# Seven-product pairs of the down projection regrouped: runs of five, one inside a body, five and three, with GpSimd's products placed behind the third body

## The chip, the cores and the metric

One core of one Trainium2 chip. The metric is the device time of one execution in microseconds; the time of a kernel is the median of its runs.

## The reference, cut to what matters

The reference is one block of a hybrid encoder on 256 rows of 2048 columns in float32. The part that the change touches is its last stage, the down projection of the gated MLP with the residual and the final norm:

```
n2 = rmsnorm(x, norm_ffn_g)
gate, up = split(n2 @ w_up, 2)              # w_up: 2048 x 11264
gate = causal_dwconv(gate, ffn_conv_w, ffn_conv_b)
x = x + (silu(gate) * up) @ w_down          # w_down: 5632 x 2048
y = rmsnorm(x, norm_final_g)
```

## The kernel before, in words

**Tiles.** The down projection multiplies an activation of 44 tiles of 128 contraction rows (`act`, 256 columns of the sequence each) by `w_down` (44 tiles x 2048 columns). It goes over two halves of 1024 output columns. All products are made of a high and a low part: ScalarE rounds a tile to the high part, VectorE subtracts it from the source and gets the low part, and TensorE multiplies high by high, high by low and low by high.

**Bodies and pairs.** Of the 44 tiles, 16 go as four *bodies* of four *units*; a unit is one tile, a load of 512 KB (128 x 1024), one rounding of 128x1024 and one of 128x256 on ScalarE, one subtraction of each on VectorE, and 12 matmuls 512 columns wide. The other 28 tiles go as 14 *pairs* of two tiles each, done as a two-by-two block product with seven products in place of eight (`pair`, L1649), so 21 matmuls of 512 columns. A pair loads three plain weight blocks (256 and 512 KB, L428 and L429) and four weight sums that an earlier stage had stored in DRAM (`sums`, 1024 KB, L436). ScalarE rounds them in four pieces (`pair_hi`: plain blocks 128x1536, activations 128x896, two pieces of sums 128x1024 each, T1 and T2), and VectorE makes the four low parts in the same order (`pair_lo`, L1222), counting `s_lo_ready`. Call the pairs of one half q0 to q13.

**Places.** There are two sets of buffers. Place 0 is a pair's own: `s_raw` for loads, `s_w` for parts of weights, `s_act` for parts of activations. Place 1 is `raw`, `w` and `aT`, which the bodies use as a ring of four slots. Each buffer is single. The plain load of the next pair at a place waits until the first low part of the pair there before is made, the load of its sums waits for all four, and ScalarE's roundings wait for TensorE (`s_used`, which a pair counts after its third and its last product).

**Order.** Everything is in program order on each engine: SyncE issues the loads, ScalarE, VectorE and TensorE work in this order for each half: body 0, q0 to q6 at places 0, 1, 0, 1, 0, 1, 0, bodies 1 and 2, q7 to q13 at places 0, 1, 0, 1, 0, 1, 0, body 3. A wait of SyncE holds back the loads behind it. The transfers of one queue share 16 DMA engines.

**Work beside it.** In the second half ScalarE makes a Sqrt table load (`warm_sqrt`) and two squares of 128x1024 (`squares`, rows 0 and 1 of the first half's columns) between bodies 1 and 2. GpSimd waits for the last product of q6 in the second half, loads `gfin` (the gain of the final norm, spread to all partitions, 1024 KB in SBUF), and makes two products of 128x512 for each of two rows (`xg`, L1414). Those of row 0 wait for the third unit of body 1, those of row 1 for the third unit of body 2. Behind the last body come `pairs_out`, the residual, and the final norm's last scalings and stores.

Of the kernel before, what the change touches and what calls it, by code (L numbers as in the profile page):

```python
# [69 lines left out]
LAST_BODY = 0, 2  # L70
# [62 lines left out]
def hybrid_block(nc, x, w_in, w_out, w_up, w_down, wa, wx, gate_w, par_in, const_in, gfin_in, out):  # L133
    with ExitStack() as ctx:
# [152 lines left out]
        def at_start(run):  # L287

            return isinstance(run, int) and run == 0

        def place_of(i):

            return i % 2

        def nth_there(half, run, i):

            return (run + half * RUNS) * ((RUN_PAIRS + 1 - place_of(i)) // 2) + i // 2

        def nth_pair(half, run, i):

            return run * RUN_PAIRS + (half * PAIRS + i)
# [53 lines left out]
        def _(sp):  # L355
# [56 lines left out]
            def load_pair(half, run, i):  # L412

                place, p = place_of(i), nth_pair(half, run, i)
# [6 lines left out]
                if i == 1:  # L421
                    g = LAST_BODY[run] + (G_DOWN + half * DOWN_BODIES)
                    sp.wait_ge(lo_ready, g * RING + (RING + 2))
                elif i:
                    sp.wait_ge(s_lo_ready, p * S_PARTS + (1 - 2 * S_PARTS))
                elif half or not at_start(run):
                    sp.wait_ge(s_lo_ready, p * S_PARTS + (1 - S_PARTS))
                sp.dma_start(dst[:, 0:BANK], upper).then_inc(plain_landed[place], 16)  # L428
                sp.dma_start(dst[:, BANK:BANK + HALF], lower).then_inc(plain_landed[place], 16)  # L429
                if i == 1:  # L430
                    sp.wait_ge(lo_ready, g * RING + 2 * RING)
                elif i:
                    sp.wait_ge(s_lo_ready, p * S_PARTS - S_PARTS)
                elif half or not at_start(run):
                    sp.wait_ge(s_lo_ready, p * S_PARTS)
# [80 lines left out]
            def load_pairs(half, run):  # L516

                for i in range(RUN_PAIRS):
                    load_pair(half, run, i)
# [19 lines left out]
        def _(act_e):  # L539
# [205 lines left out]
            def prepare_body(src, group, first, pair_before=None):  # L745

                for s in range(RING):
# [7 lines left out]
            def pair_hi(half, run, i):  # L755

                place, p, nth = place_of(i), nth_pair(half, run, i), nth_there(half, run, i)
                g = LAST_BODY[run] + (G_DOWN + half * DOWN_BODIES)
                src, dst = pair_raw[place], pair_w[place]
                act_e.wait_ge(plain_landed[place], nth * S_LOADS + S_LOADS)  # L760
                if i == 1:
                    act_e.wait_ge(unit_used, g * RING + (RING + 2))
                elif i:
                    act_e.wait_ge(s_used, p * S_STEPS + (1 - 2 * S_STEPS))
                elif half or not at_start(run):
                    act_e.wait_ge(s_used, p * S_STEPS + (1 - S_STEPS))
# [3 lines left out]
                if i == 1:  # L770
                    act_e.wait_ge(unit_used, g * RING + 2 * RING)
                elif i:
                    act_e.wait_ge(s_used, p * S_STEPS - S_STEPS)
                elif half or not at_start(run):
                    act_e.wait_ge(s_used, p * S_STEPS)
# [10 lines left out]
            def down():  # L786

                for half in range(2):
                    g0 = G_DOWN + half * DOWN_BODIES

                    for i in range(RUN_PAIRS):
                        pair_hi(half, 0, i)
                    prepare_body(act, g0 + 1, RUN_SLOTS, nth_pair(half, 0, RUN_PAIRS - 2))
                    if half == 1:
                        warm_sqrt(A4)
                        for r in range(ROWS):
                            squares(A4, r, 0, V4)
                    prepare_body(act, g0 + 2, ACT_SLOTS - 2 * RING)
                    for i in range(RUN_PAIRS):
                        pair_hi(half, 1, i)  # L800
                    prepare_body(act, g0 + 3, ACT_SLOTS - RING, nth_pair(half, 1, RUN_PAIRS - 2))
# [60 lines left out]
        def _(dve):  # L862
# [345 lines left out]
            def split_body(src, group, first, count):  # L1208

                for s in range(RING):  # L1210
# [3 lines left out]
            def pair_lo(half, run, i):  # L1214

                place, p = place_of(i), nth_pair(half, run, i)
# [30 lines left out]
            def down():  # L1247

                for half in range(2):
# [5 lines left out]
                    for i in range(RUN_PAIRS):  # L1255
                        pair_lo(half, 0, i)
                    split_body(act, g0 + 1, RUN_SLOTS, tiles + RING)
                    split_body(act, g0 + 2, ACT_SLOTS - 2 * RING, tiles + 2 * RING)
                    for i in range(RUN_PAIRS):
                        pair_lo(half, 1, i)  # L1260
# [122 lines left out]
        def _(pool):  # L1383
# [35 lines left out]
        def _(pe):  # L1419
# [191 lines left out]
            def body(where, b, **ends):  # L1611
                for s in range(RING):
# [24 lines left out]
            def pair(half, run, i, opens=False, closes=False):  # L1637

                place, p = place_of(i), nth_pair(half, run, i)
# [15 lines left out]
            def down():  # L1655

                for half in range(2):
# [8 lines left out]
                    for i in range(RUN_PAIRS):  # L1666
                        pair(half, 0, i, opens=i == 0)
# [81 lines left out]
```

## Time and profile before

| what | value |
|---|---|
| median of 3 runs | 1121.95 us (1118.27 to 1122.04) |
| the profiled execution's own time | 1120.69 us |
| its span (first to last instruction) | 1118.9 us |
| TensorE busy in the span | 1102.7 us (99%) |
| VectorE, ScalarE, GpSimd busy | 875.7, 623.9, 50.9 us |
| down projection on TensorE | 882.63 to 1108.95 us of the span |
| mean DMA rate over the span | 263 GB/s |

Times inside the span are counted from its first instruction. The span is 1.8 us shorter than the execution's own time. A matmul's end in the trace is modelled, so one instruction's length overlaps the next one's; distances between starts are what counts.

### The profile page before, as it was taken

The numbers are of one execution on the slowest core, as the hardware profiler recorded it, in microseconds if no ns is written. First come the engines' busy times: TensorE is split into PE (matmuls) and PEld (weight loads), VectorE is DVE, ScalarE is ACT, GpSimd is POOL, SyncE is SP. The second block draws the span as 40 slices with busy tenths as digits, with TensorE's granted clock in tenths as the row PEclk, the third lists the DMA queues.
The fourth block names the chain that finished last, engine by engine and source line by source line (L and its number), as shares of the span: only waits on it lengthen the run. The fifth ranks groups of instructions, "written<-read, shape, count | busy, mean of one in ns | idle before, by whom it ended". The sixth has DMA issues, their size and how long they took to land.

```text
span 1118.9 us, 16379 instructions
## 1 busy us (share of the span) xinstructions
PE 1102.7 (99%) x5938; PEld 947.1 (85%) x5938; DVE 875.7 (78%) x1144; ACT 623.9 (56%) x794; POOL 50.9 (5%) x46
## 2 busy tenths in 40 slices
PE   8999999999999999999999999999999999999996
PEld 8888888888888888888888888888888877888875
DVE  6778587685875687788788778877876897999897
ACT  7656474564755664444444444444344676867774
POOL 0100000000000000000000000000000000000200
PEclk9999999999999999999999999999999999999998
DMA  8877878678566468889889888898898898879893
GB/s 257 250 217 249 244 223 255 203 237 260 173 224 206 154 221 269 262 286 296 288 272 288 294 277 268 289 291 281 272 299 292 284 330 300 323 276 326 315 317 140
DMA packets 186727, 293.94 MB, mean 263 GB/s; under 512 B 9228, under 2 KB 151824, under 8 KB 182976
## 3 DMA queue, kind: packets, MB, share of 16 engines
q1 hardware_dynamic: 185664, 291.15, 80.1%
q0 software_dynamic: 448, 1.78, 0.5%
q10 hardware_dynamic: 576, 0.53, 0.1%
q8 instruction: 20, 0.33, 0.1%
q14 instruction: 19, 0.16, 0.0%
HBM read 261.96 MB, written 31.46 MB: 262 GB/s over the span
## 4 chain that ended last, share of the span: by engine, by line
PE 77%; DVE 10%; DMA 8%; ACT 2%; issue 1%; SPq 0%; DVEq 0%; ACTq 0%
PE ps L1465 39%; PE ps L1467 20%; PE ps L1600 10%; PE ps L1649 3%; DVE s_w L1222 3%; DVE w L868 3%; DMA s_raw<-sums 3%; DMA s_raw<-w_down_dram 2%; PE ps L1462 2%; DMA raw<-w_up_dram 1%; PE ps L1463 1%; DVE w L1222 1%; ACT w L543 1%; ACT s_w L543 1%; DMA xres<-x_dram 1%
## 5 line engine op out<-in xcount | busy, mean ns | idle before, releaser
L1465 PE MATMUL ps<-xT,w 128*128 128x512 f32 x2048 | 716.6, 396 | 0.0
L1467 PE MATMUL ps<-xT,w 128*128 128x256 f32 x2048 | 569.4, 278 | 0.0
L543 ACT ACTIVATE w<-raw 128x1024 fp32r<-128x1024 f32 (+3 forms) x377 | 392.8, 1058 | 315.7 <-PE ps L1467 151.0
L868 DVE TENSOR_TENSOR w<-raw,w 128x1024 fp32r<-128x1024 f32 x332 | 405.1, 1239 | 181.2 <-ACT w L543 180.5
L1465 PEld LDWEIGHTS ps<-xT,w 128*128 128x128 f32 x2048 | 384.2, 188 | 90.5
L1467 PEld LDWEIGHTS ps<-xT,w 128*128 128x128 f32 x2048 | 384.8, 188 | 0.3
L1600 PE MATMUL ps<-w,aT 128*128 128x512 f32 x768 | 175.7, 389 | 0.0
L1600 PEld LDWEIGHTS ps<-w,aT 128*128 128x128 f32 x768 | 143.9, 188 | 29.9
L1649 PE MATMUL ps<-s_w,s_act 128*128 128x512 f32 x336 | 80.1, 393 | 3.0 <-DVE s_act L1222 3.0
L1649 PEld LDWEIGHTS ps<-s_w,s_act 128*128 128x128 f32 x336 | 62.7, 188 | 18.4 <-DVE s_act L1222 5.0
L543 ACT ACTIVATE fs<-fc 128x512 f32<-128x512 f32 x22 | 13.9, 633 | 105.9 <-DVE fc L1307 105.9
L1222 DVE TENSOR_TENSOR s_w<-s_raw,s_w 128x1024 fp32r<-128x1024 f32 (+1 forms) x48 | 66.9, 1420 | 7.7 <-ACT s_w L543 7.6
L543 ACT ACTIVATE s_w<-s_raw 128x1024 fp32r<-128x1024 f32 (+1 forms) x48 | 55.8, 1194 | 17.1 <-DMA s_raw<-sums 8.9
L1649 PE MATMUL ps<-w,aT 128*128 128x512 f32 x252 | 59.5, 391 | 0.1
L1649 PEld LDWEIGHTS ps<-w,aT 128*128 128x128 f32 x252 | 47.0, 188 | 10.9 <-DVE aT L1222 1.1
L1405 POOL TENSOR_TENSOR fs<-fs,rB 128x512 f32<-128x512 f32 x22 | 29.3, 1331 | 568.3 <-ACT fs L543 568.3
L1222 DVE TENSOR_TENSOR w<-raw,w 128x1024 fp32r<-128x1024 f32 (+1 forms) x36 | 50.4, 1427 | 1.3 <-ACT w L543 1.1
L1052 DVE TENSOR_TENSOR s_raw<-s_raw 128x512 f32<-128x512 f32 x56 | 38.4, 687 | 0.7
L1307 DVE SCALAR_TENSOR_TENSOR fc<-fg,par,fc 128x256 f32<-128x256 f32 x88 | 36.7, 479 | 0.0
L1049 DVE TENSOR_TENSOR s_raw<-s_raw 128x1024 f32<-128x1024 f32 x28 | 34.1, 1218 | 0.0
L1462 PE MATMUL ps<-w,xT 128*128 128x512 f32 x96 | 34.1, 399 | 0.0
L543 ACT ACT_TABLE_LOAD x23 | 29.5, 1283 | 2.7 <-issue 2.3
(177 smaller groups left out, 629.1 us busy)
## 6 DMA issues: line engine op xcount, KB each, us to landing
raw<-w_up_dram SPq DMA_DIRECT2D x176, 512.0 KB, 5.9
raw<-w_in_dram SPq DMA_DIRECT2D x92, 512.0 KB, 4.3
s_raw<-w_down_dram SPq DMA_DIRECT2D x72, 512.0 KB, 7.8
sums<-s_raw SPq DMA_DIRECT2D x56, 512.0 KB, 6.5
raw<-w_down_dram SPq DMA_DIRECT2D x44, 512.0 KB, 6.7
raw<-w_out_dram SPq DMA_DIRECT2D x32, 512.0 KB, 4.6
s_raw<-sums SPq DMA_DIRECT2D x16, 1024.0 KB, 7.2
raw<-sums SPq DMA_DIRECT2D x12, 1024.0 KB, 7.3
```

The lines of the kernel that those rows point to most:

```text
L543: return sc.activation(out_, in_, fn, **kw)
L868: v.tensor_tensor(w[:, s, :, 1, :], raw[:, s, :].rearrange("p (c n) -> p c n", c=CH), w[:, s, :, 0, :], ALU.subtract).then_inc(lo_ready, 1)
L1049: v.tensor_tensor(t_out[:, 0:2, :], t_raw[:, 0:1, :].to_broadcast([P, 2, BANK]), t_raw[:, 1:3, :], ALU.subtract).then_inc(t_summed, 1)
L1052: v.tensor_tensor(t_out[:, n + 1, :], t_raw[:, n + 1, :], t_out[:, 2 * n - 2, :], ALU.subtract).then_inc(t_summed, 1)
L1222: v.tensor_tensor(out_, in_, hi, ALU.subtract).then_inc(s_lo_ready, 1)
L1307: did(v.scalar_tensor_tensor(out=fc[:, b, :], in0=tap, scalar=fpar(b, k), in1=fc[:, b, :], op0=ALU.mult, op1=ALU.add), V3, f"c{b}_{k}")
L1405: did(nc.gpsimd.tensor_tensor(fs[:], fs[:], rB[:].to_broadcast([P, 2, S]), ALU.mult), L3, "fs_r")
L1462: mm(full, xT[:, kt, 0, cut], w[:, s, c, :, :].rearrange("p a n -> p (a n)"), start=kt == 0, stop=False)
L1465: mm(full, w[:, s, c, 0, cut], xT[:, kt, :, :].rearrange("p a n -> p (a n)"), start=kt == 0, stop=False)
L1467: ins = mm(rest, w[:, s, c, 1, cut], xT[:, kt, 0, :], start=False, stop=kt == KT - 1)
L1600: ins = mm(ps[:, bank0 + 2 * r + n, :], aT[:, s, a_part, cut], w[:, s, 2 * n:2 * n + 2, w_part, :], start=opens and s == 0 and a_part == 0 ...
L1649: ins = mm(ps[:, bank, :], pair_act[place][:, a_part, cut], pair_w[place][:, m, w_part, :], start=opens and not plain and a_part == 0 and ...
```

## The change

The 14 pairs of a half are no longer two runs of seven. The order becomes: body 0, q0 to q4, units 0 and 1 of body 1, q5, units 2 and 3 of body 1, q6 to q10, body 2, q11 to q13, body 3. The places become 0, 1, 0, 1, 0, 0, 0, 1, 0, 1, 0, 0, 1, 0, so that q5 follows q4 at place 0, q6 follows q5 there, and q11 follows q10 there. SyncE issues the loads of all four units of body 1 ahead of those of q5 to q10. The number of pairs, units, loads and matmuls stays. In the second half the Sqrt table load and the square of row 0 now stand between the roundings of q5 and those of units 2 and 3; the square of row 1 stands behind these, ahead of q6. GpSimd's wait for the load of `gfin` keeps its count (the last product of q6), which now comes later in the half; its products of row 0 wait for unit 0 of body 2 and those of row 1 for unit 2 of body 2.

```diff
+HALF_PLACES = 0, 1, 0, 1, 0, 0, 0, 1, 0, 1, 0, 0, 1, 0
+FIRST_IN_RING = {1: 0, 7: 1, 12: 2}
+LAST_IN_RING = {1: 3, 2: 9, 3: 12}
...
+        def pair_there_before(half, q):
+            same = [n for n in range(2 * PAIRS) if n < nth_pair(half, q) and place_of(n % PAIRS) == place_of(q)]
+            return same[-1]
...                                                     (SyncE)
-                load_pairs(half, 0)
-                load_body(g0 + 1, w_down, RUN_TILES, half, nth_pair(half, 0, RUN_PAIRS - 2))
-                load_body(g0 + 2, w_down, FT - 2 * RING, half)
-                load_pairs(half, 1)
-                load_body(g0 + 3, w_down, FT - RING, half, nth_pair(half, 1, RUN_PAIRS - 2))
+                load_pairs(half, 0, 4)
+                load_body(g0 + 1, w_down, RUN_TILES, half, nth_pair(half, LAST_IN_RING[1]))
+                load_pairs(half, 5, 10)
+                load_body(g0 + 2, w_down, FT - 2 * RING, half, nth_pair(half, LAST_IN_RING[2]))
+                load_pairs(half, 11, 13)
+                load_body(g0 + 3, w_down, FT - RING, half, nth_pair(half, LAST_IN_RING[3]))
...                                                     (ScalarE; VectorE and TensorE likewise)
-                    for i in range(RUN_PAIRS):
-                        pair_hi(half, 0, i)
-                    prepare_body(act, g0 + 1, RUN_SLOTS, nth_pair(half, 0, RUN_PAIRS - 2))
+                    for q in range(0, 5):
+                        pair_hi(half, q)
+                    prepare_body(act, g0 + 1, RUN_SLOTS, nth_pair(half, LAST_IN_RING[1]), (0, 1))
+                    pair_hi(half, 5)
                     if half == 1:
                         warm_sqrt(A4)
-                        for r in range(ROWS):
-                            squares(A4, r, 0, V4)
-                    prepare_body(act, g0 + 2, ACT_SLOTS - 2 * RING)
-                    for i in range(RUN_PAIRS):
-                        pair_hi(half, 1, i)
+                        squares(A4, 0, 0, V4)
+                    prepare_body(act, g0 + 1, RUN_SLOTS, nth_pair(half, LAST_IN_RING[1]), (2, 3))
+                    if half == 1:
+                        squares(A4, 1, 0, V4)
+                    for q in range(6, 11):
+                        pair_hi(half, q)
+                    prepare_body(act, g0 + 2, ACT_SLOTS - 2 * RING, nth_pair(half, LAST_IN_RING[2]))
+                    for q in range(11, 14):
+                        pair_hi(half, q)
...                                                     (GpSimd)
-                pool.wait_ge(unit_used, (G_DOWN + DOWN_BODIES + r + 1) * RING + (RING + 3))
+                pool.wait_ge(unit_used, (G_DOWN + DOWN_BODIES + 2) * RING + (RING + 1 + 2 * r))
```

## Rows read from the trace of the kernel before

**Rows 1.** The page, busy time of each engine over the span.
```profile
PE 1102.7 (99%) x5938; PEld 947.1 (85%) x5938; DVE 875.7 (78%) x1144; ACT 623.9 (56%) x794; POOL 50.9 (5%) x46
```

**Rows 2.** Windows: stretch and its length, busy time by engine, clock, DMA share, GB/s.
```profile
893.53:929.32 35.79, 34.22 (x148) 27.36 (x147) 33.97 (x30) 28.89 (x31) 0.00 (x0) 1.00 0.90 314
929.32:951.08 21.76, 21.76 (x97) 18.02 (x96) 16.11 (x18) 11.89 (x15) 0.00 (x0) 1.00 0.92 312
951.08:984.59 33.51, 33.51 (x149) 27.60 (x147) 31.07 (x27) 27.92 (x29) 0.00 (x0) 1.00 0.86 310
1006.35:1040.69 34.34, 34.12 (x148) 27.44 (x147) 32.00 (x27) 27.75 (x29) 0.00 (x0) 1.00 0.90 312
1062.47:1097.91 35.44, 34.16 (x148) 27.35 (x147) 33.74 (x28) 28.03 (x30) 1.66 (x1) 1.00 0.89 308
```

**Rows 3.** Timeline of TensorE, pairs that it waited for: start, length, and the wait.
```profile
913.59 5.09 PE L1649 MATMUL ps<-s_w,s_act 128*128 128x512 f32 x21 [0.76 <-DVE s_act L1222]
...
924.39 5.09 PE L1649 MATMUL ps<-s_w,s_act 128*128 128x512 f32 x21 [0.81 <-DVE s_act L1222]
...
1083.05 5.08 PE L1649 MATMUL ps<-s_w,s_act 128*128 128x512 f32 x21 [1.28 <-DVE s_act L1222]
```

**Rows 4.** The chain of waits in the second half's first run: start, length.
```profile
1017.17 7.06 DMA s_raw<-sums
...
1027.74 7.36 DMA s_raw<-sums
```

**Rows 5.** DMA issues from 880 us on: count, KB each, median us to landing.
```profile
s_raw<-sums SPq DMA_DIRECT2D x15, 1024.0 KB, 7.1
...
s_raw<-w_down_dram SPq DMA_DIRECT2D x15, 512.0 KB, 7.1
s_raw<-w_down_dram SPq DMA_DIRECT2D x15, 256.0 KB, 5.3
...
act<-gfin_dram POOLq DMA_DIRECT2D x1, 1024.0 KB, 8.7
```

**Rows 6.** Line L436, loads of sums between 900 and 1050 us.
```profile
DMA to landing us min/median/max: 4.8/7.3/12.1
```

**Rows 7.** Timeline of VectorE, second half: start, length.
```profile
1032.96 1.76 DVE L1222 TENSOR_TENSOR s_w<-s_raw,s_w 128x1536 fp32r<-128x1536 f32 x1
1034.63 1.08 DVE L1222 TENSOR_TENSOR s_act<-act,s_act 128x896 fp32r<-128x896 f32 x1
1036.21 2.36 DVE L1222 TENSOR_TENSOR s_w<-s_raw,s_w 128x1024 fp32r<-128x1024 f32 x2 [0.49 <-ACT s_w L543]
1038.49 1.22 DVE L868 TENSOR_TENSOR w<-raw,w 128x1024 fp32r<-128x1024 f32 x1
1039.62 0.42 DVE L874 TENSOR_TENSOR aT<-act,aT 128x256 fp32r<-128x256 f32 x1
...
1059.50 3.46 DVE L1222 TENSOR_TENSOR s_w<-s_raw,s_w 128x1024 fp32r<-128x1024 f32 x2
1062.88 2.86 DVE L1222 TENSOR_TENSOR w<-raw,w 128x1536 fp32r<-128x1536 f32 x1
```

**Rows 8.** Timeline of ScalarE, both halves: start, length.
```profile
942.05 1.49 ACT L543 ACTIVATE s_w<-s_raw 128x1536 fp32r<-128x1536 f32 x1 [0.23 <-DMA s_raw<-w_down_dram]
...
1035.12 2.01 ACT L543 ACTIVATE s_w<-s_raw 128x1024 fp32r<-128x1024 f32 x2 [1.35 <-DMA s_raw<-sums]
1037.03 1.04 ACT L543 ACTIVATE w<-raw 128x1024 fp32r<-128x1024 f32 x1
...
1042.16 1.28 ACT L543 ACT_TABLE_LOAD   x1
...
1044.79 1.06 ACT L543 ACTIVATE act<-xres 128x1024 f32<-128x1024 f32 x1
...
1055.30 1.49 ACT L543 ACTIVATE s_w<-s_raw 128x1536 fp32r<-128x1536 f32 x1 [1.71 <-DMA s_raw<-w_down_dram]
```

**Rows 9.** Timeline of GpSimd, the second pair of products.
```profile
1060.07 4.06 POOL L1414 TENSOR_TENSOR act<-xres,act 128x512 f32<-128x512 f32 x2 [6.58 <-PE ps L1600]
```

More of the change, by code:

```diff
@@ L410, in store_sums, with load_pair @@
                     sp.dma_start(dst[part], s_raw[:, (2 + part) * HALF:(3 + part) * HALF]).then_inc(t_stored, 16)
-            def load_pair(half, run, i):
-                place, p = place_of(i), nth_pair(half, run, i)
+            def load_pair(half, q):
+                run, i = divmod(q, RUN_PAIRS)
+                place = place_of(q)
                 cols = half * HALF
@@ L514, in _, with load_pairs @@
             sp.wait_ge(t_stored, 32 * 2 * PAIRS)
-            def load_pairs(half, run):
-                for i in range(RUN_PAIRS):
-                    load_pair(half, run, i)
+            def load_pairs(half, first, last):
+                for q in range(first, last + 1):
+                    load_pair(half, q)
             for half in range(2):
                 g0 = G_DOWN + half * DOWN_BODIES
-                load_pairs(half, 0)
-                load_body(g0 + 1, w_down, RUN_TILES, half, nth_pair(half, 0, RUN_PAIRS - 2))
-                load_body(g0 + 2, w_down, FT - 2 * RING, half)
-                load_pairs(half, 1)
-                load_body(g0 + 3, w_down, FT - RING, half, nth_pair(half, 1, RUN_PAIRS - 2))
+                load_pairs(half, 0, 4)
[4 more added lines that the diff above has]
+                load_body(g0 + 3, w_down, FT - RING, half, nth_pair(half, LAST_IN_RING[3]))
                 if half == 0:
@@ L743, in _, with prepare_body @@
             head(H - 1, True)
-            def prepare_body(src, group, first, pair_before=None):
-                for s in range(RING):
+            def prepare_body(src, group, first, pair_before=None, units=range(RING)):
+                for s in units:
                     if pair_before is not None:
@@ L1206, in add_residual, with split_body, pair_lo @@
                                     xres[:, r, lo:hi], ALU.add), V, f"out{r}_{n}")
-            def split_body(src, group, first, count):
-                for s in range(RING):
+            def split_body(src, group, first, count, units=range(RING)):
+                for s in units:
                     split_units(group, [s])
                     split_tiles(src, first, count, [s])
-            def pair_lo(half, run, i):
-                place, p = place_of(i), nth_pair(half, run, i)
+            def pair_lo(half, q):
+                run, i = divmod(q, RUN_PAIRS)
+                place, p = place_of(q), nth_pair(half, q)
                 src, dst = pair_raw[place], pair_w[place]
@@ L1609, in half_unit, with body @@
                     ins.then_inc(unit_used, 1)
-            def body(where, b, **ends):
-                for s in range(RING):
+            def body(where, b, units=range(RING), **ends):
+                for s in units:
                     for r in range(ROWS):
@@ L1635, in out_products, with pair @@
                     last_body(where, OUT_BODIES - 1, late if half == 1 else None)
-            def pair(half, run, i, opens=False, closes=False):
-                place, p = place_of(i), nth_pair(half, run, i)
+            def pair(half, q, opens=False, closes=False):
+                place, p = place_of(q), nth_pair(half, q)
                 bank0 = 4 * (1 - half)
@@ L1665, in down @@
                         after(pe, V4, "out1_0")
-                    for i in range(RUN_PAIRS):
-                        pair(half, 0, i, opens=i == 0)
-                    body(where, 1)
+                    for q in range(0, 5):
+                        pair(half, q, opens=q == 0)
+                    body(where, 1, (0, 1))
+                    pair(half, 5)
+                    body(where, 1, (2, 3))
+                    for q in range(6, 11):
+                        pair(half, q)
                     body(where, 2)
-                    for i in range(RUN_PAIRS):
-                        pair(half, 1, i, closes=i == RUN_PAIRS - 1)
+                    for q in range(11, 14):
+                        pair(half, q, closes=q == PAIRS - 1)
                     if half == 0:
```

73 lines of the change are left out of this document (33 added, 40 removed).

## The prediction

> **What bounds the kernel now.** The page comes first, for the engine that fills the span: TensorE is busy 99% of it [rows 1], so a new order of the same matmuls can only win back time in which TensorE waits. The windows then say how much that is in the down projection. A run of seven pairs without any wait takes 33.51 us, 4.79 us for a pair; two bodies take 21.76 us, 2.72 us for a unit. The other three runs of seven take 35.79, 34.34 and 35.44 us [rows 2]: 2.28, 0.83 and 1.93 us too long, together 5.04 us. The change cannot win more there, and 5.04 us is 0.45% of 1121.95 us. About 0.5% is what a measurement of this kernel can tell from no change, so a gain that can be measured is nearly shut out before any step is costed.
>
> The timeline of TensorE says where the 5.04 us sit: ahead of the fifth and the seventh pair of a run, both at place 0, and the low parts of the activations come last [rows 3]. The chain of waits says why. At place 0 the loads of sums follow each other from 1017.17 to 1027.74 [rows 4]: one round of load, rounding and subtraction takes 10.57 us, while TensorE needs 9.57 us for two pairs. The load itself is 7.06 to 7.36 us of that [rows 4], against 4.8 us at the fastest [rows 6], so it queues. Two pairs load 2 x 1792 KB, 3.67 MB, which in 9.57 us is 383 GB/s; the runs of pairs get 308 to 314 GB/s at a DMA share near 0.9 [rows 2, 5]. A run of pairs therefore lives on a lead that it eats at some 1.1 us per two pairs, and a body (2 MiB in 10.88 us, 193 GB/s) gives it back.
>
> I measure this by lateness: when a pair's last low part is made, counted from the pair's start on TensorE. The next pair needs 1.67 + 1.00 us of VectorE (the distances between starts and the end of its first two low parts [rows 7]) within 4.79 us, so waits begin at a lateness of about 2.1 us. In the second half's first run it is 1.25 us at q2 (1017.17 against 1006.35 + 9.57), 2.24 at q4 and 3.5 at q6 (1038.57 against 1035.07) [rows 2, 4, 7], and the waits start behind q4.
>
> **Up to q5.** Nothing changes before q4's start except that the ring's loads beside q4 and q5 are 1024 KB ahead of the second megabyte where a pair's plain loads were 768 KB. In the first half q4 still starts at 913.59, 0.91 us later than 893.53 + 4 x 4.79 [rows 2, 3]. That wait stays. Then units 0 and 1 (5.44 us) stand where a pair (4.79 us) stood, and q5 follows at place 0 just as the seventh pair did, so the old seventh pair's dates serve for q5. First half: due at 913.59 + 4.79 + 5.44 = 923.82, old start 924.39 [rows 3], a wait of 0.57 us. Second half: due at 1006.35 + 5 x 4.79 + 5.44 = 1035.73, low part ready at 1034.63 + 1.08 = 1035.71 [rows 7], no wait. The 256 KB more cost 0 (nothing queued) to 0.8 us (0.26 MB at 312 GB/s) in each half; I take 0.2, near zero, because the extra load is queued eight microseconds ahead of q5's sums.
>
> **The table load and the square inside body 1.** In the second half they now stand between q5's last rounding and unit 2's. Before, they stood behind a body that was already prepared, and 10 us of matmuls hid them. Now ScalarE ends q5's sums at 1035.12 + 2.01 = 1037.13, the table load and the square take 2.63 us (1042.16 to the second square at 1044.79), unit 2's rounding 1.04, VectorE's two low parts 1.55 (1038.49 to 1040.04) [rows 7, 8]: unit 2 is ready at 1042.4, with the 0.2 of above at 1042.6. TensorE ends q5 at 1035.73 + 0.2 + 4.79 = 1040.7. That is a new wait of 1.9 us. It is 0 if q5's sums land after 4.8 us instead of 7.36 [rows 4, 6], and with a full 0.8 us of queueing it is still 1.9, since both sides move. I take 1.9, because q5's sums are queued behind the same loads as the seventh pair's were.
>
> The trace shows the table load as 1.28 us, with the next activation at its end [rows 8]. The Trainium skill (ScalarE: Activation LUTs, "What ACT_TABLE_LOAD costs") adds a drain of about 1.38 us to every switch; by it the new wait would be 3.3 us and the sum 1.4 us higher. The row has no such gap, and the row is used.
>
> **q6 to q10.** Place 0 has now no long pause from q0 to q10. Behind q5 the queue is short, which helps: q5's four low parts are made at 1038.57, q6's sums land between 1043.4 (4.8 us) and 1045.9 (7.36 us), and one rounding and two subtractions later (some 3.4 us) its low parts are complete between 1046.8 and 1049.3. q6 is due at 1035.73 + 4.79 + 5.44 = 1045.96, so its lateness is 0.9 to 3.4 us. Two rounds at 1.1 us each follow (q8, q10), and all above 2.1 us becomes wait: 1.0 us at the fast end, 2.3 us when the lateness starts at the threshold, which it can't pass without having waited already. I take 1.0 us in each half, since the queue has just run empty (in the second half the wait at unit 2 gives the loads more time, and the second square of 1.06 us [rows 8] takes some of it back).
>
> **The load of gfin.** It is issued when q6 has ended. Before, two bodies began there, and place 0 was merely late: its plain blocks were rounded 14.61 us after the bodies' start (1055.30 against 1040.69, which is 1006.35 + 34.34), 12.73 us in the first half without this load (942.05 against 929.32) [rows 2, 8]. Nobody on TensorE waited. Now it lands in q7 to q10, where the queue decides. It costs nothing if the lateness were below 2.1 us minus its delay, 3.3 us if its 1024 KB simply take their time at 312 GB/s [rows 2, 5]. I take the 1.9 us by which it delayed place 0.
>
> **GpSimd's products.** In the old order the second two (4.06 us) [rows 9] ran beside the low parts of the run's first two pairs: two subtractions of VectorE took 3.46 and 2.86 us where 2.36 and 1.76 are usual [rows 7], 1.1 us more each. The fifth pair of that run then came 1.28 us late [rows 3], and the run lost 1.93 us; the same run in the first half lost none [rows 2]. In the new order three pairs follow, then a body. VectorE has to make units 0 to 3 (4 x 1.48), q11 (5.0) and absorb some 3.6 us of contention in body 2's 10.88 us, coming from a lateness near 3: q11 ends up with a lateness of some 2.4, 0.3 us over the threshold. I take 0.3, with 0 and the old 1.93 as bounds. The Trainium skill (SBUF — State Buffer, "Who interferes with whom") says that a VectorE operation with two SBUF inputs and a GpSimd one that reads SBUF exclude each other for a whole instruction; the trace agrees, as 1.1 us steps rather than a general slowing show. The first half's last three pairs: no wait.
>
> **The sum.** First half: 0.91 + 0.57 + 0.2 + 1.0 = 2.7 us (now 2.28). Second half: 0.2 + 1.9 + 1.0 + 1.9 + 0.3 = 5.3 us (now 2.76). Together 8.0 against 5.04: 3.0 us more. The tail keeps its length, as GpSimd's products end more than a body ahead of their use. The profiled execution's own 1120.69 would become 1123.7; the median of the runs, 1.26 us above it, becomes 1124.9.
>
> The Trainium skill (DMA: Bandwidth & Descriptors, "Specifications") gives some 358 GB/s as one core's limit from HBM. By it a round of two pairs would be 10.25 us, the loss 0.7 in place of 1.1 us, and the sum an estimated 1.5 us lower. The windows show at most 314 GB/s in pairs.
>
> **Rivals.** (A) The forecast: new waits in the second half (square, gfin) outweigh the shorter runs; 1124.9. Chance 0.48.
> (B) The shorter runs win: sums land in 4.8 us behind each body, so unit 2 and q6 to q10 don't wait, and gfin is covered. Left are 0.91 + 0.57 and half a microsecond or so in each half, 2.5 us: 1119.4. For it: the run of seven that follows two bodies loses nothing [rows 2]. Against it: only 2.72 x 2 us of body now stand between q4, q5 and q6. Chance 0.30.
> (C) All waits go, even q4's: 1121.95 - 5.0 = 1116.9. Nothing before q4 changes, which speaks against it. Chance 0.07.
> (D) Slower by more than 0.5%: gfin's megabyte meets a queue with no slack, every later load of q7 to q10 is 3.3 us late and both rounds fall to 2.3 us of wait, and the lateness carries into q11, which then loses the 1.9 us again. 1.7 + 2.3 in the first half, 0.2 + 1.9 + 2.3 + 3.3 + 1.9 in the second: 13.6 us, 8.6 more, 1130.5. It decides once q10's sums land more than some 2.6 us later than in A. Chance 0.15.
>
> So the range is 1118.0 to 1129.0. Faster by over 0.5% (below 1116.3) needs C and luck: 0.04. Slower by over 0.5% (above 1127.6) is most of D: 0.14. Within 0.5%: 0.82.
>
> **What would show it.** In the profile after: q4 of the first half waiting as before; TensorE idle ahead of unit 2 of body 1 in the second half, released by a low part that waited for ScalarE; waits in q8 to q10 larger in the second half than in the first, with a load of sums of over 8 us beside gfin; no wait ahead of q13 in the second half. The prediction is wrong if the second half's q5 to q10 pass without waits, or if place 0, which now carries q4, q5 and q6 in a row, waits for its own roundings where I found them covered.

## Result: 0.3% slower, and the profile after

| | runs | median us | range us |
|---|---|---|---|
| kernel before | 12 | 1119.64 | 1116.62 to 1122.04 |
| changed kernel | 12 | 1121.69 | 1120.22 to 1126.30 |

The ratio is 1.0031, 95% interval [1.0017, 1.0045], so 3.5 us more; the two medians themselves are 2.1 us apart. A second set of runs of the same kernel gave 1.0042 [1.0025, 1.0058]. That is clear of noise and within half a per cent. The profiled execution took 1120.22 us with a span of 1118.4 us, a little less than before's. The page's span doesn't show the loss: in this execution the down projection took 1.8 us longer, but the stages ahead happened to end 1.8 us sooner, and what follows body 3's start took 20.4 us in place of 21.0.

The page of the changed kernel, the engines' busy time, answers to [rows 1]:
```profile
PE 1100.9 (98%) x5938; PEld 946.9 (85%) x5938; DVE 875.8 (78%) x1144; ACT 623.8 (56%) x794; POOL 51.5 (5%) x46
```
The same instructions, the same busy time. Only windows over the down projection show a difference. The columns are those of [rows 2]; the stretches are q0 to q4, body 1 with q5 in it, and q6 to q10 of the first half; body 1 with q5, q6 to q10, and q11 to q13 of the second:
```profile
891.77:915.71 23.94, 23.94 (x106) 19.72 (x105) 22.84 (x20) 18.28 (x19) 0.00 (x0) 1.00 0.94 333
915.71:932.22 16.51, 15.98 (x71) 12.87 (x69) 12.78 (x12) 11.39 (x13) 0.00 (x0) 1.00 0.71 249
932.22:957.07 24.85, 24.22 (x106) 19.64 (x105) 22.55 (x20) 20.74 (x22) 0.00 (x0) 1.00 1.00 368
...
1028.04:1044.53 16.49, 15.97 (x71) 12.82 (x70) 11.34 (x11) 15.11 (x19) 0.00 (x0) 1.00 0.75 262
1044.53:1072.70 28.17, 24.70 (x107) 19.44 (x105) 24.41 (x22) 20.94 (x23) 0.58 (x1) 1.00 0.95 340
...
1083.58:1097.97 14.39, 14.39 (x64) 11.83 (x63) 14.39 (x13) 12.33 (x15) 1.77 (x1) 1.00 0.65 221
```
Five pairs without a wait take 23.94 us, a pair with four units 15.67 us. The second and third stretch of each half carry it: 0.84 and 0.91 us lost in the first half, 0.82 and 4.23 us in the second. Read the DMA columns with them. Around q5 the DMA engines are 0.71 busy and move 249 GB/s, where two whole bodies had 0.92 and 312 GB/s [rows 2]; in the five pairs behind, they are 1.00 busy and move 368 GB/s. So the pause inside body 1 is used only in part for loading, and the run behind it starts a queue that is full at once. The queue of SyncE shows why. Between the load of q5's sums and the first load of q6 it issues nothing for 8.2 us, because q6 needs q5's buffer and q5's first low part is ready only at 920.79:
```profile
912.63 0.33 SPq L436 DMA_DIRECT2D s_raw<-sums  x1
920.82 0.33 SPq L430 DMA_DIRECT2D s_raw<-w_down_dram  x1
```

The timeline of TensorE, start, length and wait:
```profile
921.85 5.09 PE L1657 MATMUL ps<-s_w,s_act 128*128 128x512 f32 x21 [0.53 <-DVE s_act L1226]
...
952.14 5.09 PE L1657 MATMUL ps<-s_w,s_act 128*128 128x512 f32 x21 [0.63 <-DVE s_act L1226]
...
1038.98 5.71 PE L1608 MATMUL ps<-w,aT 128*128 128x512 f32 x24 [0.52 <-DVE aT L877]
...
1062.83 5.04 PE L1657 MATMUL ps<-w,aT 128*128 128x512 f32 x21 [3.29 <-DVE aT L1226]
```
These are q5 and q10 of the first half, unit 2 of body 1 and q9 of the second half. The waits of [rows 3] at the seventh and the fifth pair are gone; these stand in their place. The timeline of ScalarE has the causes of the last two:
```profile
1033.75 1.28 ACT L544 ACT_TABLE_LOAD   x1
...
1035.16 1.04 ACT L544 ACTIVATE act<-xres 128x1024 f32<-128x1024 f32 x1
...
1036.20 1.04 ACT L544 ACTIVATE w<-raw 128x1024 fp32r<-128x1024 f32 x1
...
1038.71 1.04 ACT L544 ACTIVATE act<-xres 128x1024 f32<-128x1024 f32 x1
...
1058.49 1.49 ACT L544 ACTIVATE w<-raw 128x1536 fp32r<-128x1536 f32 x1 [2.36 <-DMA raw<-w_down_dram]
```
Unit 2 is rounded only at 1036.20, behind table load and square. q9's plain blocks are rounded only at 1058.49: their load is the late one. That load, 512 KB issued at 1048.35, took 10.1 us to land. DMA issues between 1049 and 1060 us, columns as in [rows 5]:
```profile
act<-gfin_dram POOLq DMA_DIRECT2D x1, 1024.0 KB, 10.1
raw<-sums SPq DMA_DIRECT2D x1, 1024.0 KB, 9.7
```
q9's sums took 9.7 us beside `gfin`, against the usual 7.1 to 7.3 [rows 5, 6]. (L1226 is the low parts of pairs, [rows 7]'s L1222; L1657 and L1608 are the matmuls of pairs and units.)

**How the loss is counted below.** From q0's start to body 3's start on TensorE, less the same work without waits, 88.78 us (14 x 4.787 + 8 x 2.72). All executions, by the starts in their timelines:

| execution | order of the half | first half lost | second half lost |
|---|---|---|---|
| before, shown above | old, old | 2.28 | 2.78 |
| before_again | old, old | 0.93 | 1.55 |
| before_products_early | old, old | 0.83 | 2.74 |
| before_gfin_at_q2 | old, old | 2.23 | 3.89 |
| changed | new, new | 1.79 | 5.09 |
| after_again | new, new | 1.72 | 5.34 |
| gfin_small | new, new | 2.73 | 3.38 |
| gfin_at_q4 | new, new | 2.97 | 3.17 |
| squares_late | new, new | 2.60 | 3.06 |
| both_moved | new, new | 2.79 | 3.14 |
| first_half_only | new, old | 3.28 | 2.56 |
| second_half_only | old, new | 0.99 | 5.45 |
| runs_5333 | own, own | 1.21 | 6.72 |
| sums_halved | new, new | 0.04 | 1.02 |

An execution's first half doesn't depend on what is changed in the second, so the first column holds five samples of the old order (mean 1.45, 0.83 to 2.28) and seven of the new one (mean 2.55, 1.72 to 3.28; sums_halved, which loads less, is not among them). The means differ by 1.1 us, with a standard error of some 0.4 us. One trace is one sample of a quantity that scatters by over 1 us, and most of the readings below rest on one trace of their kernel.

### The profile page after: what moved, and what is told of

The parts are those of the page before. It is cut to its first block, busy times and chain, and to the rows that moved or that the text cites. A ratio compares the mean times of both kernels' runs of the same rounds, so it can differ in the third digit from the quotient of the medians.

```text
span 1118.4 us, 16379 instructions
## 1 busy us (share of the span) xinstructions
PE 1100.9 (98%) x5938; PEld 946.9 (85%) x5938; DVE 875.8 (78%) x1144; ACT 623.8 (56%) x794; POOL 51.5 (5%) x46
## 4 chain that ended last, share of the span: by engine, by line
PE 80%; DVE 9%; DMA 7%; ACT 2%; SPq 1%; issue 0%; DVEq 0%; ACTq 0%
PE ps L1473 42%; PE ps L1475 21%; PE ps L1608 11%; DVE s_w L1226 3%; DVE w L1226 2%; DMA s_raw<-w_down_dram 2%; PE ps L1470 2%; PE ps L1657 2%; DMA raw<-w_down_dram 2%; DMA raw<-sums 1%; PE ps L1471 1%; DVE w L871 1%; ACT s_w L544 1%; DMA xres<-x_dram 1%; ACT w L544 1%; DVE s_act L1226 1%
## 5 line engine op out<-in xcount | busy, mean ns | idle before, releaser
L544 ACT ACTIVATE w<-raw 128x1024 fp32r<-128x1024 f32 (+3 forms) x371 | 385.8, 1056 | 309.5 <-PE ps L1475 166.3
L1608 PE MATMUL ps<-w,aT 128*128 128x512 f32 x768 | 176.4, 389 | 0.5 <-DVE aT L877 0.5
L1608 PEld LDWEIGHTS ps<-w,aT 128*128 128x128 f32 x768 | 143.8, 188 | 30.7 <-DVE w L871 0.9
L1657 PE MATMUL ps<-s_w,s_act 128*128 128x512 f32 x378 | 90.1, 393 | 1.3 <-DVE s_act L1226 1.2
L1657 PEld LDWEIGHTS ps<-s_w,s_act 128*128 128x128 f32 x378 | 70.6, 188 | 18.3 <-DVE s_act L1226 2.3
L1226 DVE TENSOR_TENSOR s_w<-s_raw,s_w 128x1024 fp32r<-128x1024 f32 (+1 forms) x54 | 75.5, 1425 | 12.3 <-ACT s_w L544 12.2
L544 ACT ACTIVATE s_w<-s_raw 128x1024 fp32r<-128x1024 f32 (+1 forms) x54 | 62.8, 1194 | 22.4 <-DMA s_raw<-w_down_dram 11.9
L1657 PE MATMUL ps<-w,aT 128*128 128x512 f32 x210 | 49.3, 390 | 3.3 <-DVE aT L1226 3.3
L1657 PEld LDWEIGHTS ps<-w,aT 128*128 128x128 f32 x210 | 39.3, 188 | 11.9 <-DVE aT L1226 3.7
L1226 DVE TENSOR_TENSOR w<-raw,w 128x1024 fp32r<-128x1024 f32 (+1 forms) x30 | 42.2, 1432 | 5.7 <-ACT w L544 5.7
```

The source lines that it names most:

```text
L544: return sc.activation(out_, in_, fn, **kw)
L1226: v.tensor_tensor(out_, in_, hi, ALU.subtract).then_inc(s_lo_ready, 1)
L1608: ins = mm(ps[:, bank0 + 2 * r + n, :], aT[:, s, a_part, cut], w[:, s, 2 * n:2 * n + 2, w_part, :], start=opens and s == 0 and a_part == 0 ...
L1657: ins = mm(ps[:, bank, :], pair_act[place][:, a_part, cut], pair_w[place][:, m, w_part, :], start=opens and not plain and a_part == 0 and ...
```

## Experiments

Each was timed in five rounds beside the kernel before, and profiled once. Sections of two kernels show the edit of each against its base, the changed kernel unless the name says before.

**after_again, before_again.** Both kernels once more.

> The changed kernel once more, for a second trace and for the scatter. Loss means the time from q0's start to body 3's start on TensorE, less 88.78 us (14 x 4.787 + 8 x 2.72). In the first trace it is 1.79 us in the first half and 5.09 us in the second, of which 3.3 us is one wait ahead of q9. Theory (the load of gfin in the middle of q7 to q10 costs what its megabyte takes): the second half again loses 4.5 to 5.5 us with one wait of about 3 us ahead of q9. Rival (that wait was a chance of one execution, as the first half's wait at q4 was): the second half loses 2 to 4 us and no wait is over 1.5 us. Time: 1 to 5 us over the kernel before.

Measured: 1.72 and 5.34 us lost, a wait of 2.48 us ahead of q9 in the second half. A further 1.7 us are lost inside q9, whose matmuls take 6.49 us from start to start (1062.71 to 1069.20) because its sums landed only after 9.5 us. From q8's start to q10's this trace lost 4.4 us, the first one 4.1. The theory holds, the wait belongs to the kernel.

> The kernel before once more, for a second trace and the scatter of this chip. In its first trace the loss from q0's start to body 3's start is 2.28 us in the first half and 2.78 us in the second. Theory (the waits belong to the order): the same waits at the seventh pair of the first runs and at the fifth pair of the second half's second run, 1.5 to 3 us in each half. Rival (scatter of the DMA queue): one half loses less than 0.8 or more than 4 us.

Measured: ratio 1.0002 [0.9992, 1.0012]; 0.93 and 1.55 us lost. There are two waits of half a microsecond, ahead of the seventh pair of the first half's first run, as in the first trace, and ahead of the seventh pair of the second half's second run, where the first trace had its wait at the fifth:
```profile
1090.05 5.09 PE L1649 MATMUL ps<-s_w,s_act 128*128 128x512 f32 x21 [0.51 <-DVE s_act L1222]
```
One half lies inside the theory's range and the other, at 0.93, below it but above the rival's 0.8; the order has its waits, but this execution lost 2.48 us in all where the first had lost 5.06. The trace that the prediction rests on was at the upper end.

**gfin_small, gfin_at_q4: the load of gfin.**
```diff
-            pool.dma_start(gfin, gfin_in.to_broadcast([P, D])).then_inc(gfin_landed, 16)
+            pool.dma_start(gfin[:, 0:64], gfin_in[:, 0:64].to_broadcast([P, 64])).then_inc(gfin_landed, 16)
```


> The changed kernel, but the load of gfin brings 64 of 2048 columns at the same place (32 KB in SBUF in place of 1024 KB), so the final gain is wrong in the rest of the columns; all else is the same. Theory (queue): the wait ahead of q9 goes, the second half loses 5.1 - 3.3 = 1.8 us, the time is that of the kernel before or up to 1.5 us less. Rival (lateness: place 0 has too little pause, and gfin only moved the wait to q9): the second half still loses 3.5 us or more, spread over q8 to q10, and the time falls by less than 1 us against the changed kernel.

Measured: ratio 1.0026 [1.0013, 1.0038], the second half lost 3.38 us. Its timeline still has q9:
```profile
1062.42 5.05 PE L1657 MATMUL ps<-w,aT 128*128 128x512 f32 x21 [1.94 <-DVE aT L1226]
```
The megabyte is 1.9 us of the 5.3 us lost (mean of the three executions with it, 5.09, 5.34 and 5.45), not 3.3. The theory fails by its number (1.8 us forecast for the second half) and the rival is nearer: a wait at q9 is there without the megabyte. In time the effect is 0.05 to 0.16%, inside the intervals.

```diff
-            pool.wait_ge(s_used, S_STEPS * (PAIRS + RUN_PAIRS))
+            pool.wait_ge(s_used, S_STEPS * (PAIRS + 5))
```


> The changed kernel with the full load of gfin issued after q4's last product in place of q6's, so that it lands beside units 0 and 1 of body 1 and q5, where the queue had run nearly empty. Theory (queue slack decides): it costs q6 0 to 1 us, the 3.3 us at q9 go, the second half loses 2 to 3 us. Rival (a megabyte costs its 3.3 us wherever place 0 is near its limit, and q5 and q6 have only 5.44 us of body between them): the wait moves to q5 or q6 and the second half loses 4.5 us or more.

Measured: ratio 1.0030 [1.0015, 1.0045], 3.17 us lost in the second half, no wait at q5 or unit 2; waits of 0.43 and 0.58 us ahead of q7 and q10 instead of the long one at q9, and one of 0.60 ahead of q13. A little above the forecast of 2 to 3 us; in this trace the load costs no more around q5 than a load that is hardly there. In time it can't be told from the changed kernel.

**squares_late, both_moved: ScalarE's table load and squares.**
```diff
-                    if half == 1:
-                        warm_sqrt(A4)
-                        squares(A4, 0, 0, V4)
                     prepare_body(act, g0 + 1, RUN_SLOTS, nth_pair(half, LAST_IN_RING[1]), (2, 3))
-                    if half == 1:
-                        squares(A4, 1, 0, V4)
                     for q in range(6, 11):
                         pair_hi(half, q)
                     prepare_body(act, g0 + 2, ACT_SLOTS - 2 * RING, nth_pair(half, LAST_IN_RING[2]))
+                    if half == 1:
+                        warm_sqrt(A4)
+                        for r in range(ROWS):
+                            squares(A4, r, 0, V4)
```


> The changed kernel with the Sqrt table load and both squares behind the roundings of body 2 (10.9 us of matmuls ahead of them), none in body 1. Theory (ScalarE's order): the 0.8 us around unit 2 of body 1 go; q6's low parts come some 1 us earlier; the load of gfin still costs its wait, so the second half loses about 4.3 us and the time is 1 us less than the changed kernel. Rival (the wait at unit 2 only delayed what waits later anyway): the 0.8 us turn up at q9 and the second half loses 5.0 us as before.

Measured: ratio 1.0018 [1.0006, 1.0030], the second half lost 3.06 us, 2.2 us less than the 5.3 us with them in body 1. There is no wait at unit 2, and q6's last low part is made 0.23 us ahead of its start, where it is 1.75 us behind it in the changed kernel. So the table load and the squares cost 2.0 us of lead besides the 0.8 us wait that they show: the lead decides how long the queue's shortage can be covered. With it, q9 passes although the whole gfin is loaded, and in q6 to q10 one wait is left, ahead of q10:
```profile
1066.00 5.10 PE L1656 MATMUL ps<-s_w,s_act 128*128 128x512 f32 x21 [1.85 <-DVE s_act L1225]
```
The theory's 4.3 us and the rival's 5.0 us were both above the 3.06 us measured. The net figure also hides a part of the price. Up to body 2 the second half lost 2.2 us here against 5.3, so 3.1 us were won; the last three pairs then lost 0.9 us (15.24 us in place of 14.36), which the changed kernel doesn't lose. The squares now stand ahead of q11's roundings, and two of its low parts run beside GpSimd's products:
```profile
1079.88 4.59 DVE L1225 TENSOR_TENSOR s_w<-s_raw,s_w 128x1024 fp32r<-128x1024 f32 x2
```
That is 2.2 us more than the usual 2.36, and q12 waits.

> The changed kernel with the load of gfin after q4 and the table load and the squares behind body 2's roundings. Theory (these two are the whole loss of the change): the second half loses 1.5 to 2 us, as the first does, and the time is 1 to 2 us under the kernel before. Rival (the regrouping itself costs in the second half): it still loses 3.5 us or more.

Measured: ratio 1.0015 [0.9999, 1.0031], 2.79 and 3.14 us lost, nearer to the rival than to the theory, and the time is 1.7 us over the kernel before where the theory had it 1 to 2 us under. By one trace each (3.17, 3.06 and 3.14 us), the two moves together win no more than either one alone: with gfin's load at q4, q6's lateness is back at 1.81 us, and the lead that the squares had given is gone. The ratios (1.0030, 1.0018, 1.0015) can't tell the three apart. What is left in the second half, 3.1 us, lies near the new order's first half (2.55), where neither gfin nor squares are.

**before_gfin_at_q2, before_products_early: the old order.**
```diff
-            pool.wait_ge(s_used, S_STEPS * (PAIRS + RUN_PAIRS))
+            pool.wait_ge(s_used, S_STEPS * (PAIRS + 3))
```


> The kernel before, with the load of gfin issued after q2's last product in the second half, inside the run of seven, in place of after q6 at the start of two bodies. Theory (the megabyte costs 2 to 3.3 us wherever it is put into a run of pairs, and nothing in front of bodies): the second half's first run loses 0.83 + 2 to 3.3 us, the time is 2 to 3 us over the kernel before. Rival (the 3.3 us in the changed kernel came from q4, q5 and q6 following each other at place 0): the run loses less than 1.8 us.

Measured: ratio 1.0016 [1.0004, 1.0027]. The second half's first run takes 37.13 us (1003.93 to 1041.06) in place of 34.34 [rows 2], a loss of 3.62 us, with waits inside q5 and ahead of q6:
```profile
1032.28 3.04 PE L1649 MATMUL ps<-w,aT 128*128 128x512 f32 x12 [1.62 <-DVE w L1222]
1036.14 5.08 PE L1649 MATMUL ps<-s_w,s_act 128*128 128x512 f32 x21 [0.82 <-DVE s_act L1222]
```
In the four executions with gfin's load behind q6, this run lost 0.83, 0.20, 1.73 and 0.09 us, 0.7 on average, so the megabyte costs some 2.9 us in a run of pairs of the old order too: the theory holds for the run, while the time is 1.8 us over the kernel before (0.4 to 3.0), just under the 2 to 3 us forecast. The second run, however, then loses only 0.25 us (1062.84 to 1096.60), although GpSimd's products still run beside its first pairs:
```profile
1060.43 4.03 POOL L1414 TENSOR_TENSOR act<-xres,act 128x512 f32<-128x512 f32 x2 [7.29 <-PE ps L1600]
```

```diff
-                pool.wait_ge(unit_used, (G_DOWN + DOWN_BODIES + r + 1) * RING + (RING + 3))
+                pool.wait_ge(unit_used, (G_DOWN + DOWN_BODIES + 1) * RING + (RING + 3 + r))
```


> The kernel before, with GpSimd's products of row 1 behind the last unit of body 1 in place of the third unit of body 2, so that they run right after those of row 0, beside the preparation of body 2 and not beside q7 and q8. Theory (contention of GpSimd's products with VectorE cost the second half's second run 1.93 us): this run loses 0 to 0.6 us and the time is 1.5 to 2 us under the kernel before. Rival (the run was late because its first loads had been behind gfin's): the run still loses 1.5 us or more although its subtractions have their usual length.

Measured: ratio 0.9997 [0.9985, 1.0009], no gain where 1.5 to 2 us were forecast. The second run still loses 1.0 us (1061.11 to 1095.62), between theory and rival, with all four products done 5 us before it begins:
```profile
1090.69 5.08 PE L1649 MATMUL ps<-s_w,s_act 128*128 128x512 f32 x21 [0.54 <-DVE s_act L1222]
```
With both the load of gfin ahead and the products beside it, this second run lost 1.93, 1.33 and 2.45 us (the kernel before twice, and first_half_only). With the products and without the load ahead it lost 0.25 us, with the load and without the products 1.0 us. Each of the last two is one trace, against a scatter of 1 us; but that the products alone cost the run its 1.93 us is not borne out. The traces put some half of it on them and more on the load, so that the megabyte is not free in front of bodies either. (Moving the load also put 3 us of waits into the run ahead; what these gave the second run in lead is not separated.)

**first_half_only, second_half_only: the new order in one half.** The orders, places and waits come from a list for each half (S0 and S1 are the squares, the table load goes with S0). The lists of first_half_only:
```diff
+ORDERS = ("p0 p1 p2 p3 p4 u4 u5 p5 u6 u7 p6 p7 p8 p9 p10 u8 u9 u10 u11 p11 p12 p13 u12 u13 u14 u15",
+          "p0 p1 p2 p3 p4 p5 p6 u4 u5 u6 u7 S0 S1 u8 u9 u10 u11 p7 p8 p9 p10 p11 p12 p13 u12 u13 u14 u15")
+PLACES = (0, 1, 0, 1, 0, 0, 0, 1, 0, 1, 0, 0, 1, 0), (0, 1, 0, 1, 0, 1, 0, 0, 1, 0, 1, 0, 1, 0)
```


> The new order in the first half alone; the second half, its squares and GpSimd's load and products as in the kernel before. Over the executions so far the first half lost 2.28, 0.93, 0.83 and 2.23 us in the old order (mean 1.6) and 1.79, 1.72, 2.73, 2.97, 2.60 and 2.79 us in the new one (mean 2.4). Theory (place 0 has no long pause from q0 to q10, so the wait only moves from the seventh pair to q10): the first half loses 2 to 3 us with a wait ahead of q10, the time is 0.5 to 1.5 us over the kernel before. Rival (the regrouping costs nothing; all the loss is gfin and the squares, in the second half): no more than 1.6 us lost there, time as before.

Measured: ratio 1.0002 [0.9987, 1.0016], 3.28 us lost in the first half, waits at q5, q7 and q9:
```profile
937.35 5.10 PE L1692 MATMUL ps<-w,aT 128*128 128x512 f32 x21 [0.90 <-DVE aT L1266]
...
948.15 5.09 PE L1692 MATMUL ps<-w,aT 128*128 128x512 f32 x21 [0.77 <-DVE aT L1266]
```
The trace says what the theory says, and a little more than its 3 us, though at q7 and q9 and not at q10; the time says the rival's. The interval reaches to 1.8 us, so the 1.1 us between the means of the table is not excluded, nor shown by the times.

> The old order in the first half, the new one with its squares and GpSimd's work in the second. Theory: the second half loses 5 us as in the two traces of the changed kernel (5.09 and 5.34), the first 0.8 to 2.3 us; the time is 2 to 3 us over the kernel before, most of the change's 3.5 to 4.5 us. Rival (half of the change's cost is the first half's): 1 to 1.5 us over.

Measured: ratio 1.0039 [1.0020, 1.0059], 0.99 and 5.45 us lost. By the times the slowdown is the second half's: 4.4 us, above the 2 to 3 us that the theory gave it, with an interval from 2.2 to 6.6.

**runs_5333: another grouping.** The edit against second_half_only, whose second half has the new order; the first half's list gets the same order.
```diff
-ORDERS = (... "p0 p1 p2 p3 p4 u4 u5 p5 S0 u6 u7 S1 p6 p7 p8 p9 p10 u8 u9 u10 u11 p11 p12 p13 ..."
+ORDERS = (... "p0 p1 p2 p3 p4 u4 u5 u6 p5 p6 p7 u7 u8 u9 S0 S1 p8 p9 p10 u10 u11 p11 p12 p13 ..."
-            pool.wait_ge(s_used, S_STEPS * (PAIRS + 7))
+            pool.wait_ge(s_used, S_STEPS * (PAIRS + 8))
-                pool.wait_ge(unit_used, unit_count(1, (8, 10)[r]))
+                pool.wait_ge(unit_used, unit_count(1, (10, 11)[r]))
```


> Both halves regrouped to body 0, q0 to q4, three units, q5 to q7, three units, q8 to q10, two units, q11 to q13, body 3, with the places 0 1 0, 0 1 0, 0 1 0 in the later runs; the squares and the load of gfin in the second gap of three units. Lateness theory (a round of 10.6 us at place 0 against 9.57 us between its pairs, 12.95 us across three units, 10.2 across two): lateness grows by at most some 2.1 us before a gap takes it back, against 3.1 in the old order and 4.8 in the changed one, so the first half loses 0 to 0.8 us and the time is 0 to 2 us under the kernel before. Rival (DMA supply of the whole stretch decides, not where the pauses stand): both halves lose as in the old order or more, the time is that of the kernel before or over it.

Measured: ratio 1.0048 [1.0032, 1.0064], so 5.4 us over the kernel before where the theory allowed 2: the rival has the time right. The first half lost 1.21 us, as little as the old order's mean and above the forecast; the second lost 6.72 us. The chain of waits there begins with the table load (1048.90) and the squares ahead of q8 and runs through q8, q10 and q11 of place 0:
```profile
1056.25 7.91 DMA s_raw<-w_down_dram
...
1067.86 7.56 DMA s_raw<-w_down_dram
...
1076.97 2.48 DVE s_w L1266
1079.46 2.10 DVE s_act L1266
1081.55 4.48 DVE s_w L1266 x2
```
Here GpSimd's products do cost time: q11's first two low parts take 4.6 us where 2.67 are usual, and TensorE waits for them. In this trace the contention is paid where the lead is gone.

**sums_halved: less to load.**
```diff
-                sp.dma_start(dst[:, 2 * HALF:4 * HALF], sums).then_inc(sums_landed[place], 16)
+                sp.dma_start(dst[:, 2 * HALF:3 * HALF], sums[:, 0:HALF]).then_inc(sums_landed[place], 16)
```


> The changed kernel with the loads of sums cut to their first half (512 KB of 1024 KB for each pair), so two of the four sums of each pair are stale data and the output is wrong; all other work stays. A round of two pairs then needs 2.62 MB in 9.57 us, 274 GB/s. Theory (the DMA queue makes the lateness): all waits go, both halves lose under 0.5 us each, the time is 5 to 6.5 us under the changed kernel, 2 to 3 us under the one before. Rival (VectorE's 4.95 us for a pair against TensorE's 4.79 makes them): each half still loses 1.5 us or more.

Measured: 1116.01 us, ratio 0.9985 [0.9975, 0.9995], 5.7 us under the changed kernel's median, where 5 to 6.5 were forecast. The windows over both halves:
```profile
892.47:981.29 88.82, 88.82 (x391) 73.22 (x390) 81.86 (x76) 69.46 (x75) 0.00 (x0) 1.00 0.77 254
1003.05:1092.85 89.80, 89.18 (x391) 73.06 (x390) 80.81 (x72) 72.81 (x81) 14.09 (x5) 1.00 0.73 250
```
All the waits of the first half are gone, with the same work on VectorE and ScalarE. That is the theory; the rival (VectorE) falls. The second half keeps 1.02 us, twice the theory's bound, 0.62 of it ahead of q10; the squares and gfin's load still stand there. The scatter shrinks as well: 1115.18 to 1117.45 over twelve runs, against 1120.22 to 1126.30.

## Why the prediction was right, and where it was not

**The time.** The change was forecast at 3.0 us more and measured at 3.5. The forecast of the median itself, 1124.9 us, is 3.2 us above the measured 1121.69, inside its range; most of that is the base, since the three runs of the kernel before had a median of 1121.95 us and the twelve have 1119.64.

**What bounds the kernel**, the DMA queue behind a lead: right. sums_halved takes away only bytes and the first half's waits with them. That a gain over 0.5% was shut out was right too, and more so than it looked: the kernel before lost 2.5 us in its second trace. The lead's size was not right. The prediction put the start of waits at a lateness of 2.1 us, reckoned from VectorE's own work. But q9 of the first half was late by only 1.86 us, and q10 still waited. VectorE stood idle ahead of q10, and ahead of q9 in the second half, for plain blocks whose loads landed late (ScalarE waited 1.70 us for q10's and 2.36 us for q9's):
```profile
949.32 1.76 DVE L1226 TENSOR_TENSOR s_w<-s_raw,s_w 128x1536 fp32r<-128x1536 f32 x1 [0.87 <-ACT s_w L544]
1060.01 1.76 DVE L1226 TENSOR_TENSOR w<-raw,w 128x1536 fp32r<-128x1536 f32 x1 [2.43 <-ACT w L544]
```
In these two waits it is the landing of the plain load that decides, not VectorE's work behind a threshold.

**Up to q5**: forecast 0.91 at q4 ("That wait stays"), which the changed kernel's traces don't have. q4 starts on time in six of the seven first halves in the new order, and in three of the five in the old one; the wait belonged to the execution and not to the order. Forecast 0.77 at q5, measured 0.72 in the first trace (921.85 against 910.90 + 10.23 = 921.13), but 0 to 0.5 ahead of q5 in the six others, so that agreement is luck. In the second half 0.2 forecast, 0 measured.

**Table load and squares**: forecast a wait of 1.9 us at unit 2, measured 0.8 us (q6 starts 11.05 us behind q5 in place of 10.23), because q5's sums were rounded by 1033.73, 0.25 us behind q5's start, where the old seventh pair's dates had put that 1.4 us behind it. The mechanism was right, and its whole price larger than its wait: 2.2 us net by squares_late, 3.1 us up to body 2. That 2.2 lies near the 1.9 forecast is luck: the wait was less than half of it, and the term was sized by what TensorE shows at the spot rather than by the lead that it takes. The drain of some 1.38 us that the Trainium skill (ScalarE: Activation LUTs, "What ACT_TABLE_LOAD costs") adds to a table load does not show here either: the next activation starts at 1035.05, 1.30 us behind the load's start.

**q6 to q10**: forecast 1.0 us in the first half, measured 0.91. Lateness at q6, q8, q10 was 0.31, 1.73 and 2.73 us: less than forecast at q6 (0.9 us at the least). But the rounds of place 0 took longer than the 10.57 us of the prediction: from one low part of the sums to the next, 10.99 us (930.17 to 941.16) and 11.35 us (941.16 to 952.51), so 1.4 and 1.8 us of lead went in place of 1.1 a round. The two errors cancel.

**gfin**: forecast 1.9 us, measured 1.9 us by gfin_small, one trace against three, in a quantity that scatters by 1 us; the old order's run put the megabyte at 2.9. Together with q6 to q10 of the second half the forecast was 2.9 us and the first trace has 4.23. The rest fits the lead that the squares take, since with them moved this stretch loses 2.1 us (26.08 in place of 23.94).

**GpSimd's products**: forecast 0.3 us of new loss and the old 1.93 us gone. New loss 0 in the changed kernel: VectorE's low parts of q11 and q12 are stretched beside the products just as [rows 7] were,
```profile
1076.50 2.19 DVE L1226 TENSOR_TENSOR s_w<-s_raw,s_w 128x1536 fp32r<-128x1536 f32 x1 [0.63 <-ACT s_w L544]
1078.61 2.19 DVE L1226 TENSOR_TENSOR s_act<-act,s_act 128x896 fp32r<-128x896 f32 x1
1080.73 3.46 DVE L1226 TENSOR_TENSOR s_w<-s_raw,s_w 128x1024 fp32r<-128x1024 f32 x2
1084.11 2.85 DVE L1226 TENSOR_TENSOR w<-raw,w 128x1536 fp32r<-128x1536 f32 x1
```
and q11 to q13 lose nothing. The likely reason is the long wait at q9, in which the loads, ScalarE and VectorE catch up. Where q9 passes without it, in squares_late, both_moved and gfin_at_q4, the last three pairs lose 0.9, 0.7 and 0.9 us, and in each a stretch of two low parts takes 4.6 us beside the products. So the cost that was forecast at 0.3 us is there once nothing covers it. How much of it is the products' in the first two, where the moved squares delay q11 as well, is not separated. The step "that the products cost the old run 1.93 us" failed, however, by both old-order experiments. It did no harm to the sum, since the run's loss was entered as measured.

**The sum**: first half 2.7 us forecast, 2.55 us on average over seven executions; second half 5.3 us forecast, 5.3 us over three. The agreement is better than its parts in both halves. In the first, the 0.91 us at q4 never came, and waits that nobody forecast, ahead of q7 or inside q5, stand in for it in four of the seven. In the second, the parts erred both ways (unit 2 and q11 too high, q6 to q10 too low). The other side of the difference was the weak one: the old order's 5.04 us came from one trace, and over its executions it loses 1.45 + 2.30 = 3.7 us (the second half's mean is over the three executions with gfin and products where they were, or with no more than the first half changed). So the forecast of 3.0 us more should have been 4; the times say 3.5 and 4.7 (1.0031, 1.0042).

**What stays open**: how much the regrouping costs by itself in the first half. The traces say 1.1 us, the times of first_half_only 0.2 us, with an interval from -1.5 to 1.8 us.

## What to carry to other kernels

Before regrouping work so as to shorten the runs that outrun a queue, look at whether the pause can be used: with single buffers the loads of the next pairs could not be issued in much of it, and around q5 the queue moved 249 GB/s where it moved 312 in one unbroken stretch of two bodies. Price a small piece of work in a tight stretch by the lead that it takes, not by the wait beside it: two of them may each look like the culprit, and here, by one trace each, moving both won no more than moving one. A long wait can also hide a cost behind it that comes out when the wait is removed. And when the whole loss at stake is a few microseconds of queueing, take more than one trace, and more than three runs, of the kernel before as the baseline.

## What the runs showed of the hardware

The 16 DMA engines moved 368 GB/s at a share of 1.00 over 25 us of pairs, where [rows 2] had suggested a limit near 314; those runs were at 0.9 of the time. The Trainium skill (DMA: Bandwidth & Descriptors, "Specifications") gives some 358 GB/s as the limit from HBM for one core; the window measured here is above it, and the measurement decides. And the scatter of this kernel's times comes largely from waits on this queue: with 512 of each pair's 1792 KB gone, the spread of twelve runs fell from 6.1 to 2.3 us.
